# Two chained transformer blocks on one core: mixer layers reordered, one stream of differential attention, tables and copies released by other events

## Chip, cores and metric

One NeuronCore of a Trainium2 chip runs the whole program. The metric is the device time of one execution in microseconds, the median of several runs. Five engines work side by side, each through its own instructions in order: TensorE (PE; matmuls, with PEld for its weight loads), VectorE (DVE), ScalarE (ACT), GpSimd (POOL) and SyncE (SP), which here issues most of the DMAs. They meet through semaphores that the kernel sets and waits for by hand. TensorE's granted clock has two levels here, 2.4 GHz (1.00 in the profile) and 1.2 GHz (0.50).

## The reference, cut to what matters

Four layers run in a row over an image of 512 tokens and a context of 256, 1024 features each. Layer 0 is windowed attention with a sink, layer 1 a retention, layers 2 and 3 are layers of four mixers; every layer ends in a feed-forward. The last two, which most of the change is about:

```python
z = h @ w_in                                   # nine groups of 256 columns
u = gelu(group(z, G_AU)); v = rmsnorm(gelu(group(z, G_AV)))       # mixer a
mixed = einsum('hpq,bcqhd->bcphd', ws, v) + bs ; a = u * mixed
b = group(z, G_BB) * dwconv3(group(z, G_BC) * group(z, G_BX), w)  # mixer b
c = fft2(group(z, G_CF)).real                                     # mixer c
q, k = rope(group(z, G_DQ)), rope(group(z, G_DK)); v = group(z, G_DV)
s = einsum('bqhmd,bkhmd->bhmqk', q, k_all) * DIFF_QK ** -0.5      # mixer d
p = softmax(s); o = (p[:, :, 0] - lam * p[:, :, 1]) @ v_all
x = x + gt1 * (concatenate([a, b, c, rmsnorm(o, g) * (1 - lam_init)]) @ w_out)
```

Mixer d has four heads with two score maps each. Layer 2 computes it for the image's queries over all 768 keys and for the context's queries over the 256 keys of the context; layer 3 for the image alone.

## The kernel before

Activations lie transposed, features on the partitions: X, and HH and HL, the high and low halves of the normed input (eight tiles of 768 columns). Weights come in units of 128 output features; `plan_units` numbers all units of the program. SyncE loads unit u into WR[u % 2], ScalarE's `refill` writes its high half to WH (L665), VectorE's `refill` its low half to WL (L1011), and a product is three matmuls for each of eight input tiles: high by high, high by low, low by high (`product`, L302; `product_pair`, L315, for two units that follow a norm tile by tile; `product_rows`, L328, where tokens are the output's rows). A unit may be refilled only when the product two units before is done. PSUM is four tiles PS0 to PS3 of two banks each; `bank(PS, m)` is bank m of eight.

**First attention** (`attention` in every engine's program). 96 heads, one after the other: block b of queries, head n. In step i TensorE does the scores of head i (L434), the transposes of the probabilities of head i-3 into PS2 (L445) and, each second step, the values of two heads (L458). VectorE moves scores into SBUF and takes their maximum in one pass (L1210, printed as a custom instruction) and scales the head before (L1217, L1218). ScalarE, in step i, does the exponential of head i (L806) and then the copy of the transposed head i-3 out of PS2 (L823). The transposes of the next head wait for that copy.

**Retention** (L462 on). SyncE loads the tables and the distances only after the last tile of the norm (`h_lo`), and the weights after them.

**Mixers.** `mixers(l)`: two row units for AV into six banks, each with a gelu of its own (L883); then z units 0 to 11 and the two of DK into PS0 and PS1 by turns, each copied out by ScalarE (L889); then the spatial mixing; then two row units for DV into six banks, six copies (L909); then the Fourier mixer (`features` L558, `tokens` L568). GpSimd computes rope (L1514 to L1517). VectorE's in-order part before the stream is the AV norm, gate and convolution. The tables of a mixer layer wait for `h_lo` too, and unit 2's weights stand behind them in SyncE's queue. For the context the second Fourier table is loaded over the first.

**Differential attention.** Two blocks of eight heads over 768 keys (two query tiles each) and, in layer 2, one of eight over 256 keys. Each block is a pipeline of its own that is filled and drained: scores (L601) of both maps into PS0 and PS1, maximum (L1402) and its scaling (L1403) on VectorE, exponential on ScalarE straight from PSUM (L942), probabilities on VectorE (L1408 to L1411), transposes (L610), copy (L949), values (L619). A map's bank is free for the next head when its exponential is done. Behind the last block stands a norm over each head (`rsqrt`, `newton`, L1416), whose last halves (`mix_lo` 6 and 7) the first out product waits for.

## Time and profile before

| what | value |
|---|---|
| time, median of 3 runs | 3867.3 us (3866.22 to 3876.93) |
| the profiled execution: its time, its span | 3863.78 us, 3862.2 us |
| busy: PE, PEld, DVE, ACT, POOL | 91%, 73%, 45%, 32%, 8% of the span |
| instructions | 42880 |
| first attention / retention | from 236 to 471 us / from 1107 to 1763 us |
| mixers of layer 2: up to the stream / stream and norm | from 2144 to 2368 us / to 2515 us |
| mixers of layer 3: the same | from 3147 to 3326 us / to 3430 us |

How to read it: a wait is put down to the instruction that came last of those waited for. Idle time of an engine counts only where another waits for it. Matmuls are pipelined, and one that waits for its operands can be listed as long; their starts are more telling than their durations. A timeline merges neighbours of one line, and its count (x6) tells how many; a matmul of 32-bit floats appears as two in some counts.

### The profile page before, as it was taken

The page shows a single profiled execution, that of the slowest core. Times are in us where ns is not written, and L with a number is a line of the kernel's source. Part 1 is how long each engine was busy: PE and PEld are TensorE (multiplying, and loading weights), DVE is VectorE, ACT ScalarE, POOL GpSimd, SP SyncE. Part 2 cuts the span into 40 slices and gives each one's busy share as a digit, 9 for nine tenths or more (in the row PEclk, how much of TensorE's full clock was granted, in tenths as well). Part 3 has the DMA queues.
Part 4 walks back from the last instruction along what each step waited for, and adds up shares of the span by engine and source line. Part 5 has one row for each costly group of instructions (what it writes and reads, how often), then busy time and mean ns, then how long its engine had stood idle before and what let it go on. Part 6 is the DMA issues. An engine that isn't in the chain of part 4 may idle for free.

```text
span 3862.2 us, 42880 instructions
## 1 busy us (share of the span) xinstructions
PE 3519.3 (91%) x17952; PEld 2838.3 (73%) x17952; DVE 1750.9 (45%) x2605; ACT 1224.6 (32%) x1711; POOL 292.5 (8%) x361
## 2 busy tenths in 40 slices
PE   6967789999979999998999798989999979889998
PEld 3766578888866757656888685678888867567887
DVE  3555545433333433336756325546535432555343
ACT  4455542112232221224222323432212233344232
POOL 0100010000100000001001001010000010110001
PEclk8989899999999999998999897799999989899999
DMA  5400023423211212114544210013323322012222
GB/s 204 169 19 1 1 87 126 133 86 126 91 68 46 73 39 73 62 44 140 194 152 147 84 61 17 1 71 126 136 83 126 100 72 87 11 44 80 95 98 87
DMA packets 87903, 334.23 MB, mean 87 GB/s; under 512 B 11168, under 2 KB 14240, under 8 KB 83872
## 3 DMA queue, kind: packets, MB, share of 16 engines
q1 hardware_dynamic: 66544, 252.85, 18.5%
q0 software_dynamic: 21168, 78.65, 6.2%
q8 instruction: 142, 2.33, 0.2%
q14 instruction: 49, 0.40, 0.0%
HBM read 329.37 MB, written 2.10 MB: 86 GB/s over the span
## 4 chain that ended last, share of the span: by engine, by line
PE 86%; DVE 5%; ACT 5%; issue 2%; DMA 2%; SPq 0%; POOL 0%; ACTq 0%; DVEq 0%
PE PS L302 62%; PE PS L328 5%; PE PS L523 3%; PE PS L601 2%; PE PS L496 2%; PE PS L315 2%; PE PS L619 1%; PE PS L458 1%; PE PS L488 1%; PE PS L445 1%; PE PS L434 1%; PE PS L568 1%; PE PS L610 1%; DVE aP L1210 1%; DMA AR<-in_ada 1%
## 5 line engine op out<-in xcount | busy, mean ns | idle before, releaser
L302 PE MATMUL PS<-HH,WH 128*128 128x512 f32 (+1 forms) x3120 | 943.3, 357 | 69.2 <-ACT AV L883 33.4
L665 ACT ACTIVATE WH<-WR 128x1024 fp32r<-128x1024 f32 (+1 forms) x376 | 419.2, 1115 | 1735.4 <-PE PS L302 1466.1
L302 PE MATMUL PS<-HH,WL 128*128 128x512 f32 (+1 forms) x3120 | 937.7, 355 | 0.0
L302 PE MATMUL PS<-HL,WH 128*128 128x512 f32 (+1 forms) x3120 | 937.1, 355 | 0.0
L1011 DVE TENSOR_TENSOR WL<-WR,WH 128x1024 fp32r<-128x1024 f32 (+1 forms) x376 | 486.9, 1295 | 976.2 <-ACT WH L665 975.7
L302 PEld LDWEIGHTS PS<-HH,WH 128*128 128x128 f32 x3120 | 516.3, 190 | 161.2 <-ACT AV L883 33.8
L302 PEld LDWEIGHTS PS<-HL,WH 128*128 128x128 f32 x3120 | 514.8, 189 | 86.7 <-issue 2.2
L302 PEld LDWEIGHTS PS<-HH,WL 128*128 128x128 f32 x3120 | 515.3, 189 | 85.3
L302 PE MATMUL PS<-DH,WH 128*128 128x512 f32 (+1 forms) x1056 | 318.8, 356 | 0.0
L302 PE MATMUL PS<-DL,WH 128*128 128x512 f32 (+1 forms) x1056 | 318.7, 356 | 0.0
L302 PE MATMUL PS<-DH,WL 128*128 128x512 f32 (+1 forms) x1056 | 318.6, 356 | 0.0
L1137 DVE SCALAR_TENSOR_TENSOR X<-PS,MOD,X 128x512 f32<-128x512 f32 x96 | 60.5, 658 | 368.0 <-PE PS L302 368.0
L302 PEld LDWEIGHTS PS<-DL,WH 128*128 128x128 f32 x1056 | 174.3, 188 | 29.9
L302 PEld LDWEIGHTS PS<-DH,WH 128*128 128x128 f32 x1056 | 174.1, 188 | 30.2
L302 PEld LDWEIGHTS PS<-DH,WL 128*128 128x128 f32 x1056 | 174.0, 188 | 29.9
L1042 DVE SCALAR_TENSOR_TENSOR PS<-AT,CB 128x1024 f32<-128x1024 f32 x144 | 176.5, 1226 | 0.0
L328 PE MATMUL PS<-WH,HH 128*128 128x256 f32 (+1 forms) x416 | 142.2, 342 | 28.8 <-DVE HL L1069 15.8
L1487 POOL DMA_DIRECT2D AT<-in_adat x144 | 76.0, 528 | 1148.3 <-DVE AT L1042 574.5
L1479 POOL TENSOR_TENSOR WK<-WK,WK 128x768 f32<-128x768 f32 (+1 forms) x56 | 117.0, 2089 | 329.1 <-ACT WK L681 328.6
L328 PE MATMUL PS<-WL,HH 128*128 128x256 f32 (+1 forms) x416 | 140.8, 339 | 0.0
L328 PE MATMUL PS<-WH,HL 128*128 128x256 f32 (+1 forms) x416 | 140.8, 338 | 0.0
L740 ACT ACTIVATE DH<-WK 128x768 fp32r<-128x768 f32 (+1 forms) x88 | 65.0, 739 | 185.4 <-DVE WK L1128 185.4
(261 smaller groups left out, 3872.6 us busy)
## 6 DMA issues: line engine op xcount, KB each, us to landing
WR<-in_win SPq DMA_DIRECT2D x176, 512.0 KB, 3.5
AT<-in_adat POOLq DMA_DIRECT2D x144, 512.0 KB, 3.8
WR<-in_wdn SPq DMA_DIRECT2D x64, 704.0 KB, 4.0
WR<-in_wret SPq DMA_DIRECT2D x64, 512.0 KB, 3.6
WR<-in_zin SPq DMA_DIRECT2D x36, 512.0 KB, 3.5
AR<-in_ada SPq DMA_DIRECT2D x8, 1024.0 KB, 5.5
aV<-in_ada SPq DMA_DIRECT2D x8, 1024.0 KB, 4.9
aAR<-in_ada SPq DMA_DIRECT2D x8, 1024.0 KB, 6.6
```

Source lines behind the costliest of these rows:

```text
L302: mm = PE.matmul(dst[:, a:b], w[u % 2][:, k * P:(k + 1) * P], h[:, k, a:b], start=(k == 0 and i == 0), stop=(k == nk - 1 and i == 2))
L315: mm = PE.matmul(dst[v][:, a:b], w[(u + v) % 2][:, k * P:(k + 1) * P], h[:, k, a:b], start=(k == 0 and i == 0), stop=(k == KT - 1 and i == 2))
L328: mm = PE.matmul(dst(m), h[:, k0 + k, m * P:(m + 1) * P], w[u % 2][:, k * width:(k + 1) * width], start=(first and k == 0 and i == 0), sto ...
L496: mm = PE.matmul(d, M.rV[:, m, e * P:(e + 1) * P], M.rAT[:, m, :], start=(m == 0), stop=(m == 5))
L523: mm = PE.matmul(PS[half][:, 512 * v:512 * v + 512], wt[half][:, col:col + P], y[:, k, :], start=(k == 0 and i == 0), stop=(k == 3 and i = ...
L601: mm = PE.matmul(PS[mp][:, a:e], qs[r, h // 2, q * P:(q + 1) * P], M.DK[r, h // 2, k0 + a:k0 + e], start=True, stop=True, tile_position=(r ...
L665: AC.activation(M.WH[u % 2][:, 0:n], M.WR[u % 2][:, 0:n], COPY).then_inc(*on.up("w_hi", u))
L740: AC.activation(M.DH[:, j, 0:n], HF[:, 0:n], COPY).then_inc(*on.up("d_hi", (l, jj)))
L1011: VE.tensor_tensor(M.WL[u % 2][:, 0:n], M.WR[u % 2][:, 0:n], M.WH[u % 2][:, 0:n].bitcast(F32), ALU.subtract).then_inc(*on.up("w_lo", u))
L1042: i = VE.scalar_tensor_tensor((PS[3], M.AT[v % 3])[j][:, :], M.AT[v % 3][:, :], 1.0, M.CB[:, j, :], ALU.mult, ALU.mult, accum_out=MOD[:, l ...
L1479: PO.tensor_tensor(WK[2][:, 0:n], WK[2][:, 0:n], WK[k % 2][:, 0:n], ALU.add).then_inc(*on.up("square_summed", (tag, k)))
L1487: PO.dma_start(M.AT[v % 3][:, :], dram["adat"][l - 1, v]).then_inc(*on.up(f"mod_load{v % 3}", (l, v), 16))
```

## The change

It has six parts.
- **Order of units** in the mixer layers: `MIX` gives the order of the 14 units (u, Fourier input, q and k first, the convolution's last); DV's rows come ahead of the last six, the spatial mixing after six.
- **Rows two tiles to a bank**: AV's and DV's rows use `row_place`, banks 4 to 6, so three copies of 512 columns take the place of six of 256. The gelu of u is done in the copy out of PSUM. Rope moves from GpSimd to VectorE.
- **One stream**: the differential attention's blocks become one list of heads (`diff_heads`). VectorE's pass moves the scores to SBUF and takes their extreme in one (with `NIL`, a tile of zeros, as second operand); the exponential works in place in SBUF, and a bank is free when VectorE has read it. Scores of the two maps alternate, values of two heads too. The square sums behind it move into the first out product, after its third input tile.
- **Tables** of the retention and of the mixer layers wait for the last down product (and the last ada tile) and no longer for the norm. The context's Fourier table gets space of its own, in HL's last tiles; the second context's load moves to head 1 of the retention.
- **First attention**: in each step ScalarE copies the transposed head i-3 first and then does the exponential of head i; VectorE's low halves of the output come a step later.
- The layout of the z weights follows the new order of the units.

On ScalarE, in the first attention at 640 columns a step, before (aP is the exponential, aPT the copy; the last digits are buffers, aPT_93 to aPT_96 the four of a cycle, aP_89 to aP_92 likewise):

```order
L823 ACTIVATE aPT_95<-PS 128x640 [waits a_values,a_transposed]
L806 ACTIVATE aP_91,aRSM<-aP_91,aNM 128x641 [waits a_sink,a_max]
L823 ACTIVATE aPT_96<-PS 128x640 [waits a_values,a_transposed]
L806 ACTIVATE aP_92,aRSM<-aP_92,aNM 128x641 [waits a_sink,a_max]
L823 ACTIVATE aPT_93<-PS 128x640 [waits a_values,a_transposed]
L806 ACTIVATE aP_89,aRSM<-aP_89,aNM 128x641 [waits a_sink,a_max]
```

and now (aPT_94 to aPT_97, aP_90 to aP_93):

```order
L833 ACTIVATE aPT_97<-PS 128x640 [waits a_values,a_transposed]
L840 ACTIVATE aP_92,aRSM<-aP_92,aNM 128x641 [waits a_sink,a_max]
L833 ACTIVATE aPT_94<-PS 128x640 [waits a_values,a_transposed]
L840 ACTIVATE aP_93,aRSM<-aP_93,aNM 128x641 [waits a_sink,a_max]
L833 ACTIVATE aPT_95<-PS 128x640 [waits a_values,a_transposed]
L840 ACTIVATE aP_90,aRSM<-aP_90,aNM 128x641 [waits a_sink,a_max]
```

The two kinds alternated before and do so now; what moved is the place of a step's copy, from behind the exponential of head i to ahead of it (before: aP_92 and then aPT_93, the fourth and the first buffer; now aPT_97 and then aP_92, the fourth and the third).

On SyncE's queue at the start of mixer layer 2, behind the load of its second unit, before (dBD to WS are the first four of eleven tables; the third unit's load stands behind the last of them, before and now):

```order
L1552 DMA WR_53<-in_zin 128x1024 [waits w_lo]
L1561 DMA dBD<-in_bd 128x128 [waits h_lo]
L1561 DMA SLG<-in_subln 128x1
L1561 DMA LQ<-in_lambda 128x128
L1561 DMA WS<-in_gmlp_w 128x512
```

and now:

```order
L1589 DMA WR_54<-in_zin 128x1024 [waits w_lo]
L1598 DMA dBD<-in_bd 128x128 [waits ada_taken,product]
L1598 DMA SLG<-in_subln 128x1
L1598 DMA LQ<-in_lambda 128x128
L1598 DMA WS<-in_gmlp_w 128x512
```

The order is the same; the event that the first table waits for is another.

On VectorE, one head of the stream over 768 keys, before:

```order
L1402 TENSOR_REDUCE dNM<-PS 128x1 [waits d_scores]
L1403 TENSOR_SCALAR dNM<-dNM 128x1 [waits step]
L1402 TENSOR_REDUCE dNM<-PS 128x1 [waits d_scores]
L1403 TENSOR_SCALAR dNM<-dNM 128x1 [waits step]
L1408 RECIPROCAL dRL<-dRL 128x2 [waits d_exp]
L1409 TENSOR_TENSOR dRL<-dRL,LAM 128x1 [waits step]
L1410 TENSOR_SCALAR dP_157<-dP_157,dRL 128x768
L1411 SCALAR_TENSOR_TENSOR dP_157<-dP_159,dRL,dP_157 128x768 [waits step]
```

and now (ISA is the custom pass of L1210's kind, and the reading of its result):

```order
L1450 ISA dP_158,dNM<-PS,NIL 128x768 [waits d_scores,d_prob]
L1450 ISA dNM 128x1
L1450 ISA dP_159,dNM<-PS,NIL 128x768 [waits d_scores]
L1450 ISA dNM 128x1
L1457 RECIPROCAL dRL<-dRL 128x2 [waits d_exp]
L1458 TENSOR_TENSOR dRL<-dRL,LAM 128x1 [waits step]
L1459 TENSOR_SCALAR dP_157<-dP_157,dRL 128x768
L1460 SCALAR_TENSOR_TENSOR dP_157<-dP_160,dRL,dP_157 128x768 [waits step]
```

Two maxima and two scalings became two passes that also write dP; the rest of a head is unchanged.

The diff, cut to its core (what the code above shows and the change removes, places in SBUF, gate, convolution and weight layout are left out; the pieces are, in this order, of the module, TensorE, ScalarE, VectorE and SyncE):

```diff
+MIX = (0, 1, 8, 9, 10, 11, 12, 13, 2, 6, 4, 3, 7, 5)
+ROWS_AT, MIXED_AT = 8, 6
+def mix_units(l):
+    return [(p + 2 * (p >= ROWS_AT), p, z) for p, z in enumerate(MIX)]
+def diff_heads(l):
+    return [(q, h, 6 if q < 4 else 2, 0 if q < 4 else 4) for q in range(segments(l)[-1][1] // P) for h in range(4)]
+def row_place(ps, m):
+    return bank(ps, 4 + m // 2)[:, L * (m % 2):L * (m % 2) + L]
...
+        for at, p, z in mix_units(l):
+            if p == MIXED_AT:
+                PE.wait_ge(*on("av_normed", l))
+                PE.wait_ge(*on("table", f"mixers{l}"))
+                for t in (1, 0):
+                    for h in (2 * t, 2 * t + 1):
+                        for m in range(nt):
+                            mm = PE.matmul(mixed[t][64 * (h % 2):64 * (h % 2) + 64, m * P:(m + 1) * P],
+                                           M.AV[:, m, 64 * h:64 * h + 64], M.WS[:, h, :], start=True, stop=True)
+                    mm.then_inc(*on.up("mixed", (l, t)))
+            if p == ROWS_AT:
+                for t in range(2):
+                    PE.wait_ge(*on("mix_biased", (l, t)))
+                for v in range(2):
+                    product_rows(u + 2 + ROWS_AT + v, 4, 4 * v, L, range(6), place, v == 0, v == 1, None, True)
+            product(u + 2 + at, PS[p % 2], (HH, HL), KT, segs if z < 12 else ALL, ("z_copied", (l, MIX[p - 2])) if p > 1 else None)
 
...
+        heads = diff_heads(l)
...
+                rows = [slice(64 * (h % 2) + 32 * mp, 64 * (h % 2) + 32 * mp + 32) for mp in range(2)]
+                for a in range(0, w, 512):
+                    e = min(w, a + 512)
+                    for mp, r in enumerate(rows):
+                        if j and a == 0:
+                            PE.wait_ge(*on("d_max", (l, j - 1, mp)))
+                        mm = PE.matmul(PS[mp][:, a:e], M.Z[r, 10 + h // 2, q * P:(q + 1) * P], M.DK[r, h // 2, c0 + a:c0 + e],
+                                       start=True, stop=True, tile_position=(r.start, 0))
+                        if e == w:
+                            mm.then_inc(*on.up("d_scores", (l, j, mp)))
...
+            j = step - 4
+            if j >= 0 and j % 2 == 0:
+                q, h, nm, m0 = heads[j]
...
+                for m in range(nm):
+                    for g in range(2):
+                        mm = PE.matmul(out[64 * g:64 * g + 64, :], M.DV[:, m0 + m, 64 * (h + g):64 * (h + g) + 64],
+                                       M.dPT[(j + g) % 4][:, m, :], start=(m == 0), stop=(m == nm - 1))
+                mm.then_inc(*on.up("d_values", (l, j // 2)))
...
+        def square_sums():
+            for t in range(2):
+                PE.wait_ge(*on("o_squared", (l, t)))
+                PE.wait_ge(*on("d_turned", (l, len(heads) - 1)))
+                for a, b, _ in segs:
+                    mm = PE.matmul(PS[2 + t][:, a:b], M.dBD[:, :], (M.dP[0][0], M.dP[0][1])[t][:, a:b], start=True, stop=True)
+                mm.then_inc(*on.up("o_square_sum", (l, t)))
...
+            i = step - LAG
+            if 0 <= i < HEADS:
+                w = len(keys(i // 16)) * P
+                AC.wait_ge(*on("a_transposed", i))
+                if i > 3:
+                    AC.wait_ge(*on("a_values", (i - 4) // 2))
+                AC.activation(M.aPT[i % 4][:, 0:w], PS[2][:, 0:w], COPY).then_inc(*on.up("a_turned", i))
             i = step
             if i < HEADS:
...
+        for at, p, z in mix_units(l):
+            if p == ROWS_AT:
+                for v in range(2):
+                    refill(u + 4 + ROWS_AT + v)
+                AC.wait_ge(*on("product", u + 3 + ROWS_AT))
+                for i in range(3):
+                    AC.activation(flat(M.DV, 2 * i, 2 * i + 2), bank(PS, 4 + i), COPY).then_inc(*on.up("dv_copied", (l, i)))
+            refill(u + 4 + at)
+            AC.wait_ge(*on("product", u + 2 + at))
+            dst, w = (Z[:, z, 0:n], n) if z < 12 else (M.DK[:, z - 12, :], T)
+            AC.activation(dst, PS[p % 2][:, 0:w], GELU if z < 2 else COPY).then_inc(*on.up("z_copied", (l, z)))
+            if p == 5:
+                AC.wait_ge(*on("lambda_dots", l))
+                AC.activation(M.LAM[:, 0:2], M.LAM[:, 0:2], EXP).then_inc(*on.up("lambda_exp", l))
+            if p == 11:
+                middle(0)
...
+        heads = diff_heads(l)
+        for step in range(len(heads) + 4):
+            j = step - 3
+            if 0 <= j < len(heads):
+                nm = heads[j][2]
+                AC.wait_ge(*on("d_transposed", (l, j)))
+                if j > 3:
+                    AC.wait_ge(*on("d_values", (l, (j - 4) // 2)))
+                AC.activation(M.dPT[j % 4][:, 0:nm, :], PS[2][:, 0:nm * P].rearrange("p (a b) -> p a b", b=P),
+                              COPY).then_inc(*on.up("d_turned", (l, j)))
+            j = step
+            if j < len(heads):
+                w = heads[j][2] * P
+                for mp in range(2):
+                    p = M.dP[mp][j % (3 - mp)][:, 0:w]
+                    AC.wait_ge(*on("d_max", (l, j, mp)))
+                    AC.activation(p, p, EXP, bias=M.dNM[:, j % 4, mp:mp + 1], scale=-1.0,
+                                  accum_out=M.dRL[:, j % 4, mp:mp + 1]).then_inc(*on.up("d_exp", (l, j, mp)))
...
+        def rope(t):
+            q, rt, before = Z[:, 10 + t, 0:S] if t < 2 else M.DK[:, t - 2, 0:S], RT[:, :], {1: 0, 2: 1, 3: 2}.get(t)
+            VE.wait_ge(*on("z_copied", (l, 10 + t)))
+            if before is not None:
+                VE.wait_ge(*on("roped", (l, before)))
+            step(VE.stream_shuffle(rt, q, [i ^ 8 for i in range(32)]), ("rope_swapped", l, t))
+            VE.tensor_tensor(q, q, M.mCOS[:, :], ALU.mult)
+            step(VE.tensor_tensor(rt, rt, M.mSIN[:, :], ALU.mult), ("rope_sin", l, t))
+            VE.tensor_tensor(q, q, rt, ALU.add).then_inc(*on.up("roped", (l, t)))
...
+        for at, p, z in mix_units(l):
+            if p == ROWS_AT:
+                refill(u + 4 + ROWS_AT)
+                rope(2)
+                refill(u + 5 + ROWS_AT)
+                rope(3)
+            refill(u + 4 + at)
+            if p == 2:
+                lambda_dots()
+            if p == 5:
+                gate()
+            if p == 6:
+                rope(0)
+                lambda_rest()
+            if p == 7:
+                rope(1)
+            if p == 11:
+                conv(0)
...
+        for at in range(len(heads) + 1):
+            j = at
+            if j < len(heads):
+                w = heads[j][2] * P
+                if j > 2:
+                    VE.wait_ge(*on("d_transposed", (l, j - 3)))
+                if j > 1:
+                    VE.wait_ge(*on("d_prob", (l, j - 2)))
+                for mp in range(2):
+                    VE.wait_ge(*on("d_scores", (l, j, mp)))
+                    VE.tensor_tensor_reduce(M.dP[mp][j % (3 - mp)][:, 0:w], PS[mp][:, 0:w], M.NIL[:, 0:w], -(32 ** -0.5), 3e38,
+                                            ALU.add, ALU.min, M.dNM[:, j % 4, mp:mp + 1]).then_inc(*on.up("d_max", (l, j, mp)))
...
-    SP.wait_ge(*on("h_lo", ("1a", KT - 1)))
-    SP.dma_start(M.X[:, :, S:T], dram["xc2"].rearrange("p (k t) -> p k t", k=KT)).then_inc(*on.up("x_load", 1, 16))
+    SP.wait_ge(*on("product", FIRST["down", 0, 1] + KT - 1))
+    SP.wait_ge(*on("ada_taken", (1, NV - 1)))
...
+        if h == 1:
+            SP.wait_ge(*on("h_lo", ("1a", KT - 1)))
+            SP.dma_start(M.X[:, :, S:T], dram["xc2"].rearrange("p (k t) -> p k t", k=KT)).then_inc(*on.up("x_load", 1, 16))
...
-        SP.wait_ge(*on("h_lo", (f"{l}a", KT - 1)))
+        SP.wait_ge(*on("product", FIRST["down", l - 1, 1] + KT - 1))
+        SP.wait_ge(*on("ada_taken", (l, NV - 1)))
...
-            SP.wait_ge(*on("dft_tokens", (l, 0, 1)))
-            SP.dma_start(M.CN[:, :, 0, :], dram["dft256"]).then_inc(*on.up("dft", (l, 1), 16))
+            SP.wait_ge(*on("product", u + 17))
+            SP.dma_start(M.CC[:, :, :, :], dram["dft256"].rearrange("p q (m k) -> p q m k", m=2)).then_inc(*on.up("dft", (l, 1), 16))
```

## Rows read from the trace of the kernel before

**Rows 1.** Waits of TensorE, whole span: line <- releaser: us in total, times, longest.

```profile
PE PS L445 <- ACT aPT L823: 63.1, 54, 2.8
...
PE PS L302 <- ACT AV L883: 33.4, 2, 18.5
...
PE PS L558 <- ACT DV L909: 13.2, 2, 7.0
...
PE PS L302 <- DVE HL L1378: 7.9, 3, 4.1
...
PE PS L568 <- DMA CN<-in_dft: 2.7, 1, 2.7
```

**Rows 2.** Timeline, first attention: start, us, engine, line, out<-in, count [idle before <-releaser].

```profile
321.20 0.73 PE L445 MATMUL PS<-aID,aP 128*128 128x128 f32 x5
...
321.69 0.89 PE L434 MATMUL PS<-aK,aQS 128*128 128x256 f32 x6
...
322.33 0.83 ACT L806 ACTIVATE aP<-aP,aNM 128x641 f32<-128x641 f32 x1 [2.32 <-DVE aNM L1210]
...
323.16 0.68 ACT L823 ACTIVATE aPT<-PS 128x640 f32<-128x640 f32 x1
...
323.99 0.74 PE L445 MATMUL PS<-aID,aP 128*128 128x128 f32 x5 [1.41 <-ACT aPT L823]
...
324.66 1.31 PE L458 MATMUL PS<-aPT,aV 128*64 128x128 f32 x20
...
326.66 0.73 PE L445 MATMUL PS<-aID,aP 128*128 128x128 f32 x5
```

**Rows 3.** Timeline, start of the retention.

```profile
1141.19 1.06 ACT L665 ACTIVATE WH<-WR 128x1024 fp32r<-128x1024 f32 x1 [11.55 <-DMA WR<-in_wret]
...
1143.56 1.01 PE L302 MATMUL PS<-HH,WH 128*128 128x512 f32 x2 [11.21 <-DVE WL L1011]
```

**Rows 4.** Timeline, end of layer 1's feed-forward and SyncE's tables.

```profile
2142.76 0.75 DVE L1137 SCALAR_TENSOR_TENSOR X<-PS,MOD,X 128x512 f32<-128x512 f32 x1 [5.32 <-PE PS L302]
...
2167.91 0.33 SPq L1561 DMA_DIRECT2D dBD<-in_bd  x1
```

**Rows 5.** Chain that ended last, mixer layer 2: start, us, what.

```profile
2173.51 10.58 DMA WR<-in_zin
...
2392.00 2.87 PE PS L601 x8
...
2394.87 1.47 PE PS L610 x6
...
2396.34 2.75 PE PS L619 x12
```

**Rows 6.** Timeline, differential attention of layer 2, at full clock.

```profile
2408.25 0.96 DVE L1402 TENSOR_REDUCE dNM<-PS 128x1 f32<-128x768 f32 x1 [2.22 <-PE PS L601]
...
2408.95 1.52 PE L619 MATMUL PS<-dPT,DV 128*64 128x128 f32 x12
...
2409.31 0.95 DVE L1402 TENSOR_REDUCE dNM<-PS 128x1 f32<-128x768 f32 x1
...
2412.21 0.95 DVE L1402 TENSOR_REDUCE dNM<-PS 128x1 f32<-128x768 f32 x1
```

**Rows 7.** Windows: stretch, length, busy of PE PEld DVE ACT POOL, granted clock, DMA.

```profile
2368.00:2420.00 52.00, 46.24 (x192) 29.68 (x191) 32.29 (x67) 23.34 (x43) 0.00 (x0) 0.67 0.00 0
...
2420.00:2470.00 50.00, 45.93 (x201) 29.99 (x200) 31.39 (x64) 21.84 (x42) 0.00 (x0) 0.69 0.00 1
...
2470.00:2515.00 45.00, 37.73 (x160) 23.97 (x158) 24.25 (x72) 21.01 (x53) 0.00 (x0) 0.71 0.00 1
...
3326.00:3375.00 49.00, 43.64 (x216) 28.68 (x216) 32.26 (x66) 22.60 (x43) 0.00 (x0) 0.79 0.00 0
...
3375.00:3430.00 55.00, 46.81 (x225) 31.53 (x225) 35.94 (x72) 28.58 (x51) 0.00 (x0) 0.84 0.00 1
```

**Rows 8.** VectorE groups, first attention: busy us, mean ns | idle before.

```profile
L1210 DVE CUSTOM_DVE_ANT_0 aP<-PS,aMK,aSK 128x640 f32<-128x640 f32 x32 | 28.2, 881 | 32.3 <-PE PS L434 32.2
```

More of the change, by code:

```diff
@@ L289, in tensor_program, with product @@
     PS, HH, HL, WH, WL = M.PS, M.HH, M.HL, M.WH, M.WL
-    def product(u, dst, src, nk, segs, after=None, ready=None):
+    def product(u, dst, src, nk, segs, after=None, ready=None, between=None):
         PE.wait_ge(*on("w_lo", u))
@@ L297, in product @@
         for k in range(nk):
+            if between and k == 3:
+                between()
             if ready:
@@ L318, in product_pair, with product_rows @@
                     mm.then_inc(*on.up("product", u + v))
-    def product_rows(u, nk, k0, width, tiles, dst, first, last, ready=None):
+    def product_rows(u, nk, k0, width, tiles, dst, first, last, ready=None, paired=False):
         PE.wait_ge(*on("w_lo", u))
@@ L328, in product_rows @@
                 mm = PE.matmul(dst(m), h[:, k0 + k, m * P:(m + 1) * P], w[u % 2][:, k * width:(k + 1) * width],
-                               start=(first and k == 0 and i == 0), stop=(last and k == nk - 1 and i == 2))
+                               start=(first and k == 0 and i == 0 and not (paired and m % 2)),
+                               stop=(last and k == nk - 1 and i == 2 and not (paired and m % 2 == 0)))
         mm.then_inc(*on.up("product", u))
@@ L530, in mixers @@
         u = FIRST["zin", l]
+        place = lambda m: row_place(PS, m)
         for v in range(2):
-            product_rows(u + v, 4, 4 * v, L, range(nt), lambda m: bank(PS, m)[:, 0:L], v == 0, v == 1,
-                         ("h_lo", f"{l}a"))
-        PE.wait_ge(*on("av_gelu", (l, nt - 1)))
-        for i in range(12):
-            product(u + 2 + i, PS[i % 2], (HH, HL), KT, segs, ("z_copied", (l, i - 2)) if i > 1 else None)
-        for i in range(2):
-            product(u + 14 + i, PS[i], (HH, HL), KT, ALL, ("z_copied", (l, 10 + i)))
@@ L549, in mixers @@
[L549 to L552 removed]
+            product_rows(u + v, 4, 4 * v, L, range(nt), place, v == 0, v == 1, ("h_lo", f"{l}a"), True)
+        mixed = [PS[3], PS[2]]
+        for at, p, z in mix_units(l):
[14 more added lines that the diff above has]
+            product(u + 2 + at, PS[p % 2], (HH, HL), KT, segs if z < 12 else ALL, ("z_copied", (l, MIX[p - 2])) if p > 1 else None)
@@ L622, in mixers @@
-        last = 2 if n > S else 1
-        for t in range(2):
-            PE.wait_ge(*on("o_squared", (l, t)))
-            PE.wait_ge(*on("d_out", (l, last, 1)))
-            PE.wait_ge(*on("d_turned", (l, last, 7)))
-            for a, b, _ in segs:
-                mm = PE.matmul(PS[2 + t][:, a:b], M.dBD[:, :], (M.dP[0][0], M.dP[0][1])[t][:, a:b], start=True, stop=True)
-            mm.then_inc(*on.up("o_square_sum", (l, t)))
+                tokens(t, S, lambda q, m: M.CC[:, q, m, :], 2, L)
@@ L958, in mixers @@
-        last = 2 if n > S else 1
+        heads = diff_heads(l)
+        for step in range(len(heads) + 4):
+            j = step - 3
+            if 0 <= j < len(heads):
+                nm = heads[j][2]
[4 more added lines that the diff above has]
+                              COPY).then_inc(*on.up("d_turned", (l, j)))
+            j = step
+            if j < len(heads):
[5 more added lines that the diff above has]
+                                  accum_out=M.dRL[:, j % 4, mp:mp + 1]).then_inc(*on.up("d_exp", (l, j, mp)))
+            j = step - 5
+            if j >= 0 and j % 4 == 2:
+                q = heads[j][0]
+                AC.wait_ge(*on("d_values", (l, j // 2)))
+                AC.activation(M.OD[:, :, q * P:(q + 1) * P], bank(PS, 6 + q % 2)[:, 0:2 * P].rearrange("p (t q) -> p t q", t=2),
+                              COPY).then_inc(*on.up("d_out", (l, q)))
@@ L959, in mixers @@
         N = [*M.dP[0], M.dP[1][0]]
-        AC.wait_ge(*on("d_out", (l, last, 1)))
+        AC.wait_ge(*on("d_out", (l, heads[-1][0])))
         for t in range(2):
@@ L1200, in attention @@
             stack(0, g)
-        for at in range(HEADS + LAG + 4):
+        for at in range(HEADS + LAG + 5):
             i = at
@@ L1233, in retention @@
         T1, T2, DC, TMP, DS = M.rAT[:, 0, :], M.rAT[:, 1, :], M.rDC[:, :], M.rTMP, M.rDS
-        VE.wait_ge(*on("table", "retention"))
-        VE.memset(M.rON[:, :], 1.0 / 512).then_inc(*on.up("step", "rON"))
         def rope(h, what, pa, pb, dst):
@@ L1250, in retention @@
             VE.wait_ge(*on("product", u + 1))
+            if h == 0:
+                VE.wait_ge(*on("table", "retention"))
+                VE.memset(M.rON[:, :], 1.0 / 512).then_inc(*on.up("step", "rON"))
             rope(h, 0, PS[0], PS[1], M.rQ)
```

278 lines of the change are left out of this document (84 added, 194 removed).

## The prediction

> **What bounds the kernel now.** I read the waits of TensorE first: they say where it stands still and which instruction ended each wait. Four lines hold most of it: 63.1 us in the first attention behind ScalarE's copies at L823, 33.4 us at the starts of the two mixer layers behind the gelu of AV, 13.2 us behind the copies of DV, 2.7 us behind a table; 7.9 us at the heads of the out projections come on top [rows 1]. Then the timeline of each place, for what is really late there. Last the windows, because TensorE's granted clock is not the same everywhere: in the differential attention it is 0.67 to 0.71 of full speed on average in layer 2 and 0.79 to 0.84 in layer 3 [rows 7], that is, one part of the stretch at 1.2 GHz and the rest at 2.4.
>
> **First attention: copies first.** At 321.20 TensorE transposes a head's probabilities, done at 321.93. The copy that frees their bank starts only at 323.16, since on ScalarE the exponential of a later head (322.33) stands ahead of it. The next transposes wait 1.41 us for that copy and start at 323.99 [rows 2]. In the changed order the copy can start at 321.95 and ends after its 0.68 us at about 322.65; the scores in between end at 322.58. So the transposes start at about 322.7 instead of 323.99: 1.28 of 1.41 us go, 91%. What is delayed is the exponential, from 322.33 to 322.67. Its result is wanted three heads later, and two heads now take 5.46 us (321.20 to 326.66 [rows 2]), so it has 8 us and, at the new pace, still 6: nothing. If that cover were gone, 0.34 us a head would come back, 33 us for 96 heads. 91% of 63.1 is 57 us. I take off 7 for the ten places where ScalarE stacks queries between copies, whose delay stays. **-50**, bounds -40 and -60. VectorE's low halves, one step later, lie in the same slack.
>
> **Retention.** The tables are loaded after the norm, the next weights queue behind them, ScalarE gets those only at 1141.19 after 11.55 us of idle time, and TensorE stands 11.2 us until 1143.56 [rows 3]. The changed queue waits for the last down product (and the last ada tile, which is earlier) instead, so all of it lands under the norm. What is late next is the conversion of that unit, which needs the buffer that the first product of the pair frees: 1.06 us on ScalarE [rows 3] and about as long on VectorE, against some 0.7 us of matmuls of the pair's other half that are left by then. So about 1.5 us of wait stay. **-10** (bounds -8 and -12). The 1 MB load of the second context moves to head 1, ahead of that head's weights on SyncE's queue; those are wanted two products later, some 10 us: 0 to +2, and I take 0.
>
> **Mixers up to the streams.** The same with the norms of layers 2 and 3: the down product ends just before 2142.76, the tables start at 2167.91 [rows 4], and the next weights land 10.6 us after their issue at 2173.51 [rows 5]. On the new condition all of this is 25 us sooner, and the weights land near 2159, ahead of the norm's end (where the tables start now). The gelu no longer stands between rows and units either: rows go two tiles to a bank into PS2 and PS3, units into PS0 and PS1. The 33.4 us go but for a microsecond. DV's rows come ahead of six units and their three copies lie under those; the 13.2 us become the copy of the last unit, 1 us a layer. The context's table has its own space in HL's tail: -2.7. Rope on VectorE (a shuffle and three passes over 512 columns, each 0.65 us by the 0.96 of a maximum over 768 [rows 6]) is 2.6 us beside a conversion of about 1.1; a unit has 24 matmuls at least, 6 us at full clock by the 1.01 us that two take at half of it [rows 3]. It fits, and so do gate and convolution: nothing. After each of the vanished waits the matmuls now restart at half clock (that same row), which I price at 6 together. 33.4 + 13.2 + 2.7 - 3 + 6: **-52** (bounds -45 and -58).
>
> **Differential attention.** At 1.2 GHz a head costs TensorE 2.87 us for scores, 1.47 for transposes and 2.75 for values, 7.1 in all [rows 5], and VectorE waits. At 2.4 GHz the values take 1.52 and VectorE is the bound: it starts heads at 2408.25 and 2412.21, 3.96 us apart [rows 6]. The pass that replaces maximum and scaling also moves the scores to SBUF. The trace has it at 640 columns as 881 ns [rows 8], so 1.06 us or a little less at 768; from one maximum to the next it is 1.06 now (2408.25 to 2409.31). VectorE's work for a head stays at 4.0 to 4.1. What goes is its idle time at starts and ends of blocks, and half of TensorE's time for values, since two heads now run side by side, as in the first attention (1.31 us for 20 instructions [rows 2], so 1.6 for 24).
> At 2.4 GHz throughout, a layer then costs VectorE's busy time, one start, one end and the norm behind it. Layer 2: 147 us from 2368 to 2515, busy 32.3+31.4+24.3 = 88, idle 59 [rows 7]. Of the idle time there stay, as estimates, 5 at the start, 2 at the end and 9 in the norm: -43. Layer 3: 104 us, busy 32.3+35.9 = 68, idle 36 [rows 7], of which 15 stay: -21.
> At 1.2 GHz two heads cost TensorE 2 x (2.87+1.47) + 3.2 = 11.9, against 8.1 on VectorE: +4 for two heads. The start, where TensorE waits for VectorE's first passes, is as long as before, so the clock will fall there as it does now. How long it stays down is the open size: the mean clocks (twice what is missing from 1, times the length) say 34, 31 and 26 us in layer 2's three windows, 21 and 18 in layer 3's two. I take one such stretch a layer, 25 us or two pairs: +8 each. **-35** and **-13**; bounds -43 and -8, -21 and +11.
> That values of two heads side by side gain anything goes against a rule of the Trainium skill (TensorEngine Tiling (Array Packing), PSUM Bottleneck): tiling speeds up the matmuls but not the emptying of PSUM, which can become the bound. At 2.4 GHz the rows above are that case; at 1.2 GHz they are not, TensorE being the full engine. By the rule alone a pair at 1.2 GHz would keep its 14.2 us, and the time would be 3716.
> The square sums now stand behind three steps of the first out product instead of ahead of it. The 7.9 us at its head [rows 1] wait for the norm on ScalarE and VectorE, which the move doesn't shorten: 0 to +1, and I take 0.
>
> **Sum.** -50-10-52-35-13 = -160, against the profiled execution's 3863.8 (span 3862.2): 3704. The median of the runs is 3867.3, 3.5 above it, so 3707. Errors of 10, 2, 6, 12 and 12 that don't hang together make this case 3687 to 3727.
>
> **Rivals.** (1) The streams stay at 1.2 GHz from start to end. For it: layer 2's windows are more than half at that level, the one with the context's block too [rows 7]. Against: layer 3's heads wait on VectorE in the same way and run two thirds of the time at full speed. Layer 2 then keeps -43+4x8+3 = -8 and layer 3 -21+4x8 = +11: instead of -48 it is +3, time 3758. The Trainium skill (TensorE: Matmul & The Clock Gate, HAM oscillation) says that a kernel whose matmuls come in bursts between waits falls back to the lower rate again and again; by that rule this is the case to expect.
> (2) In the first attention the exponential, now behind the copy, is late, and the wait for the copy turns into one for probabilities: 33 us come back, 3740. Against it: the three heads of lead.
> (3) The clock stays at 2.4 GHz in both streams: 16 us better, 3691. For it: one start a layer instead of two or three. Against: the start itself.
> (4) Slower than before: copy ahead of exponential ties each head to the one before it. Then a head costs a whole chain: scores 0.89, reduction 0.88, exponential 0.83, transposes 0.73, copy 0.68 [rows 2, 8] and, as an estimate, 0.9 for reading the sum and scaling, 4.9 us in all against 2.73 now (half of 5.46); +2.2 at 640 columns, on average perhaps 1.6, so +155 for 96 heads instead of -50: 3912. It decides from the point where one head's chain is longer than the three heads of lead, 6 us at the new pace. It is 4.9.
>
> **How the numbers follow.** Forecast 0.64, (1) 0.14, (2) 0.10, (3) 0.09, (4) 0.03. The range goes from (3) with some error to (1): 3682 to 3758. About 0.3% (12 us) is what a measurement here can tell from no change; all cases but (4) are far beyond it, and only several losses together would end there: faster 0.95, same 0.02, slower 0.03.
>
> **What would show it.** In the first attention the waits for the copies fall from 63 to under 12 us, and no other wait of TensorE there passes 10. No wait over 2 us at the start of the retention, and none over 2 between a mixer's rows and its stream. In each stream one stretch of about 25 us at half clock, then heads 4.0 to 4.2 us apart with VectorE busy throughout. Wrong would be: half clock to the end of a stream; heads of 5 us at full clock (a dearer pass); conversions of weights that come late because VectorE turns rope or convolves first.

## The result and the profile after

The changed kernel takes 3691.6 us in the median (3685.3 to 3699.4, four runs), the kernel before 3871.0 beside it: a ratio of 0.9537, interval 0.9508 to 0.9565. Measured again with other runs it is 3691.3 and 0.9536 (0.9512 to 0.9559). The profiled execution has a span of 3684.0 us against 3862.2. Times below are medians, and "over" or "under" is against 3691.3 unless something else is named; the kernel before, measured beside each group of runs, took 3867.6 to 3868.4 us.

The span is 178.2 us shorter. The stretches, from the starts and ends of the matmuls in the two traces:

| stretch | before, us | after, us | change | forecast |
|---|---|---|---|---|
| first attention, first scores to first out product | 234.6 | 171.2 | -63.4 | -50 |
| from the last down product to the retention's product of [rows 3] | 38.2 | 29.1 | -9.2 | -10 |
| rest of the retention | 617.5 | 612.9 | -4.5 | 0 |
| mixers, last down product to first scores, layers 2 and 3 | 226.9 + 181.2 | 197.0 + 148.6 | -62.5 | -52 |
| first scores to end of the out product, layer 2 | 207.2 | 177.1 | -30.2 | -35 |
| the same, layer 3 | 144.8 | 136.2 | -8.6 | -13 |
| all else | | | +0.2 | 0 |

Waits of TensorE after the change, whole span (line <- releaser: us in total, times, longest), where [rows 1] has 63.1, 33.4, 13.2, 7.9 and 2.7:

```profile
PE PS L470 <- ACT aPT L833: 12.4, 38, 1.1
...
PE PS L326 <- DVE HL L1427: 11.0, 4, 3.3
PE PS L632 <- ACT dPT L969: 10.7, 9, 3.4
...
PE PS L326 <- DVE WL L1037: 5.4, 3, 2.1
...
PE PS L581 <- ACT Z L931: 1.9, 2, 1.0
```

The waits for AV, DV and CN are gone altogether; in the place of DV's 13.2 stand 1.9 for the last unit's copy, and the retention starts after a wait of 2.1 for its weights (the longest in the fourth line) instead of 11.2. The waits inside the first out products, 7.9 before, are 11.0 now. Of the signs that the prediction named, two are missed by a little: the copies' 12.4 is not under 12, and the retention's 2.1 not under 2. Between a mixer's rows and its stream no wait is over 1.0. The timeline of the first attention after, two heads at 640 columns (start, us, engine, line):

```profile
302.61 0.73 PE L470 MATMUL PS<-aID,aP 128*128 128x128 f32 x5
...
303.37 0.71 ACT L833 ACTIVATE aPT<-PS 128x640 f32<-128x640 f32 x1 [1.15 <-PE PS L470]
...
303.97 0.82 ACT L840 ACTIVATE aP<-aP,aNM 128x641 f32<-128x641 f32 x1
...
304.22 0.74 PE L470 MATMUL PS<-aID,aP 128*128 128x128 f32 x5 [0.23 <-ACT aPT L833]
...
306.88 0.73 PE L470 MATMUL PS<-aID,aP 128*128 128x128 f32 x5
```

The copy (L833) now starts when the transposes (L470) end, the exponential (L840) follows it, and the next transposes wait 0.23 us instead of 1.41 [rows 2]. Two heads take 4.27 us instead of 5.46.

The windows of the two streams after (the columns of [rows 7]; the granted clock is the third figure from the end):

```profile
2262.00:2288.00 26.00, 24.53 (x94) 13.92 (x94) 17.59 (x39) 12.19 (x24) 0.00 (x0) 0.61 0.00 0
2288.00:2352.00 64.00, 56.01 (x381) 35.21 (x381) 52.94 (x144) 40.61 (x94) 0.00 (x0) 0.89 0.00 1
3156.00:3182.00 26.00, 24.05 (x91) 13.57 (x90) 17.75 (x38) 12.41 (x24) 0.00 (x0) 0.61 0.00 0
3182.00:3230.00 48.00, 41.05 (x268) 25.78 (x266) 39.77 (x88) 29.47 (x58) 0.00 (x0) 0.88 0.00 1
```

Each stream starts with one stretch of 20 us at half clock (2 x 0.39 x 26). Behind it the clock is mostly full but not always: 0.89 of 64 us and 0.88 of 48 are another 14 and 12 us at half. VectorE's passes there, at full clock:

```profile
2287.88 0.96 DVE L1450 CUSTOM_DVE_ANT_0 dP<-PS,NIL 128x768 f32<-128x768 f32 x1 [2.98 <-PE PS L620]
...
2288.76 0.95 DVE L1450 CUSTOM_DVE_ANT_0 dP<-PS,NIL 128x768 f32<-128x768 f32 x1
...
2291.71 0.96 DVE L1450 CUSTOM_DVE_ANT_0 dP<-PS,NIL 128x768 f32<-128x768 f32 x1
...
2295.62 0.96 DVE L1450 CUSTOM_DVE_ANT_0 dP<-PS,NIL 128x768 f32<-128x768 f32 x1 [0.22 <-PE PS L620]
```

Heads are 3.83 and 3.91 us apart, a little under the 4.0 to 4.1 of the prediction: from one pass to the next it is 0.88 us, where a maximum with its scaling took 1.06 [rows 6]. That holds only at full clock; where it has fallen, a head comes up to 5.8 us after the one before it.

### The profile page after: what moved, and what is told of

The parts are those of the page before. It is cut to its first block, busy times and chain, and to the rows that moved or that the text cites. A ratio compares the mean times of both kernels' runs of the same rounds, so it can differ in the third digit from the quotient of the medians.

```text
span 3684.0 us, 42824 instructions
## 1 busy us (share of the span) xinstructions
PE 3449.4 (94%) x17952; PEld 2782.0 (76%) x17952; DVE 1743.7 (47%) x2627; ACT 1214.7 (33%) x1696; POOL 255.6 (7%) x337
## 4 chain that ended last, share of the span: by engine, by line
PE 89%; DVE 4%; ACT 4%; issue 1%; DMA 1%; SPq 0%; POOL 0%; DVEq 0%; ACTq 0%
PE PS L326 65%; PE PS L352 6%; PE PS L548 3%; PE PS L521 2%; PE PS L339 2%; PE PS L620 1%; PE PS L470 1%; PE PS L513 1%; PE PS L483 1%; PE PS L645 1%; PE PS L459 1%; PE PS L591 1%; DMA AR<-in_ada 1%; PE PS L632 1%; DVE dP L1450 1%
## 5 line engine op out<-in xcount | busy, mean ns | idle before, releaser
L326 PEld LDWEIGHTS PS<-HH,WH 128*128 128x128 f32 x3120 | 514.6, 189 | 122.4 <-issue 16.6
```

Source lines behind the costliest of these rows:

```text
L326: mm = PE.matmul(dst[:, a:b], w[u % 2][:, k * P:(k + 1) * P], h[:, k, a:b], start=(k == 0 and i == 0), stop=(k == nk - 1 and i == 2))
```

## The experiments

**The changed kernel again** stands beside the others.

> The changed kernel itself, beside which the others are read. Every theory expects its 3691.6 us (3685 to 3699).

It took 3691.3 us. Its profile differs from the first one mainly in layer 2's stream with the out product, 183.6 us instead of 177.1, so the streams' entries in the table are good to some 6 us.

**First attention: waits or clock?** My theory was that 50 of the 63 us are waits and 13 the clock. Two runs. In the changed kernel the order put back, on ScalarE and with VectorE's low halves a step earlier again:

```diff
-            i = step - LAG
-            if 0 <= i < HEADS:
...
-                AC.activation(M.aPT[i % 4][:, 0:w], PS[2][:, 0:w], COPY).then_inc(*on.up("a_turned", i))
             i = step
...
                         "p (a b) -> p a b", b=P), COPY).then_inc(*on.up("o_hi", (b, t // 4)))
+            i = step - LAG
+            if 0 <= i < HEADS:
...
+                AC.activation(M.aPT[i % 4][:, 0:w], PS[2][:, 0:w], COPY).then_inc(*on.up("a_turned", i))
```

And in the kernel before, useless matmuls ahead of the transposes of every second head, where TensorE waited, into the place that the next values overwrite:

```diff
+                    for _ in range(6):
+                        PE.matmul(bank(PS, 6 + tt // 4)[:, tt % 4 * P:(tt % 4 + 1) * P], M.aID[:, :], M.aID[:, :], start=True, stop=True)
```

> The changed kernel with the first attention put back: in each step the exponential of head i first, then the copy of head i-3, and VectorE's low halves a step earlier. Theory: the first attention got 63 us shorter, 50 of them by the waits for the copies and 13 by TensorE's clock, which no longer falls there because TensorE no longer stands still; both come back with the order, so +63 us, the waits for copies at 60 us or more, and about 34 us at half clock between 256 and 470 us. Rival: only the waits hang on the order, and the 13 us come from another part of the change: +50 us, and no half clock in that stretch.

> The kernel before, with six matmuls of 128x128 that nobody reads in every second step of the first attention, put where TensorE waits 1.41 us for a copy. The output is unchanged. Theory (the clock gives 13 of the 63 us): two heads at 640 columns still take 5.46 us, but the stretches at half clock between 256 and 470 us go, and the kernel is 13 us faster than before, 3855. Rival (the 13 us come from shorter work per head): the time stays as before, 3867 to 3871, whatever the clock does.

With the order put back: 3758.0 us, 67 over; the first attention takes 234.5 us again, the waits for the copies are at 63.3, and the clock is back at 0.93. The windows from 256 us to near the end of the first attention: kernel before, copies last, changed kernel, before with useless matmuls:

```profile
256.00:466.00 210.00, 149.05 (x1341) 123.57 (x1339) 125.01 (x373) 124.22 (x284) 17.24 (x87) 0.93 0.00 1
```

```profile
256.00:466.00 210.00, 149.00 (x1340) 123.48 (x1338) 124.98 (x374) 124.28 (x284) 17.39 (x87) 0.93 0.00 1
```

```profile
256.00:402.00 146.00, 131.57 (x1296) 109.96 (x1292) 118.81 (x360) 117.82 (x274) 17.19 (x84) 1.00 0.01 2
```

```profile
256.00:462.00 206.00, 197.23 (x1883) 176.25 (x1883) 125.77 (x374) 124.52 (x285) 17.14 (x87) 0.99 0.01 1
```

So the whole 63 us and the clock hang on the two moves put back here, ScalarE's order and the step of VectorE's low halves; the two were not run apart. The useless matmuls raise the clock from 0.93 to 0.99 without changing the order, and 3860.9 us against 3868.4 is 0.9977 (0.9960 to 0.9994): 2 to 15 us less, 7.5 in the middle and not 13. In its trace the first attention takes 230.1 us, 4.5 less than before. The trace says why it is not more: pairs of heads that fell on half clock go from 7.02 and 7.73 us to 5.38, while at 256 columns, where the wait is shorter than six matmuls, some pairs grow, from 3.01 to 3.67. That the clock pays is shown; that it pays 13 is not. Pair by pair, steady pairs at full clock give 48 us (8 pairs each of 1.04, 1.17, 1.17, 1.06, 0.79 and 0.79 in the six blocks); some 9 more come from pairs that had been at half clock, and the rest from the pairs in which ScalarE also stacks queries (5.94 us before, 4.28 after).

**Mixer starts: weights behind tables, or gelu?**

```diff
-    SP.wait_ge(*on("product", FIRST["down", 0, 1] + KT - 1))
-    SP.wait_ge(*on("ada_taken", (1, NV - 1)))
+    SP.wait_ge(*on("h_lo", ("1a", KT - 1)))
...
-        SP.wait_ge(*on("product", FIRST["down", l - 1, 1] + KT - 1))
-        SP.wait_ge(*on("ada_taken", (l, NV - 1)))
+        SP.wait_ge(*on("h_lo", (f"{l}a", KT - 1)))
```

> The changed kernel, but the tables of the retention and of the mixer layers wait for the norm again. Theory: at the starts of the mixer layers it was the weights behind the tables that TensorE waited for, not the gelu of AV. Then the retention starts 9 us later, and from the last down product to the first unit after the rows it takes 45.5 us again instead of 31.1 (layer 2) and 26.9 (layer 3): +14 and +19, with 3 to 8 us of half clock after the waits: +45 to +50 us in all. Rival: the gelus and their six evictions were the wait, and they stay gone: only the retention's 9 us come back.

3728.3 us, 37 over. The timeline of the changed kernel with late tables, layer 2 (SPq is the DMA queue; a merged row is as long as its loads together):

```profile
2100.14 0.33 SPq L1598 DMA_DIRECT2D dBD<-in_bd  x1
...
2105.26 27.20 SPq L1589 DMA_DIRECT2D WR<-in_zin  x5
...
2115.87 1.06 ACT L692 ACTIVATE WH<-WR 128x1024 fp32r<-128x1024 f32 x1 [16.75 <-DMA WR<-in_zin]
...
2118.24 1.01 PE L326 MATMUL PS<-HH,WH 128*128 128x512 f32 x2 [12.69 <-DVE WL L1037]
...
2119.46 1.57 ACT L910 ACTIVATE AV<-PS 128x512 f32<-128x512 f32 x3
```

and of the changed kernel:

```profile
2065.04 0.33 SPq L1598 DMA_DIRECT2D dBD<-in_bd  x1
...
2070.16 28.86 SPq L1589 DMA_DIRECT2D WR<-in_zin  x4
...
2096.09 0.52 PE L326 MATMUL PS<-HH,WH 128*128 128x512 f32 x2
```

With early tables the first unit follows the rows without a wait. With late ones TensorE stands 12.7 us (16.6 in layer 3, 8.5 at the retention) for the conversion of weights that land late, and this although the gelu (L910) comes after that matmul, which does not wait for it. So 29 of the 33.4 us that [rows 1] puts down to the gelu were the weights; the gelus stood behind the conversion on ScalarE's queue and only reported last. In the kernel before, layer 2:

```profile
2182.86 1.06 ACT L665 ACTIVATE WH<-WR 128x1024 fp32r<-128x1024 f32 x1 [15.96 <-DMA WR<-in_zin]
...
2186.48 1.76 ACT L883 ACTIVATE AV<-PS 128x256 f32<-128x256 f32 x6
...
2188.29 1.01 PE L302 MATMUL PS<-HH,WH 128*128 128x512 f32 x2 [14.91 <-ACT AV L883]
```

The expected 45 to 50 were 8 to 13 too many. Some 4 of them are what the gelus and their six evictions had cost themselves: from the last down product to the first unit it now takes 43.3 and 43.7 us, not 45.5. Another 3 are the retention's, whose start comes 6.5 us later and not 9; the rest is open.

**DV's place, and the square sums.**

The first kernel moves DV's rows, the second the sums:

```diff
-ROWS_AT, MIXED_AT = 8, 6
+ROWS_AT, MIXED_AT = 13, 6
```

```diff
-        return square_sums
+        square_sums()
...
-        project(l, segments(l), mixers(l))
+        mixers(l)
+        project(l, segments(l))
```

> The changed kernel with DV's rows ahead of the last unit instead of ahead of the last six. Theory (three wide copies and any unit behind them are enough, some 2 us under 8): the same time, 3691, and no wait for DV's copies. Rival (DV's rows need the place: their copies stand behind late conversions on ScalarE, or the shuffles and passes of rope that go with them delay the last unit's conversion): a wait of 3 us or more at the start of the Fourier features in each layer, 3697 and up.

> The changed kernel with the square sums of the differential attention ahead of the first out product, as before, instead of behind its third step. Theory (the norm on ScalarE and VectorE is what the product waits for either way): the same time, 3691, within 2 us. Rival (three steps of the product, 3 to 5 us, are now done while the squares are made): +3 us a layer or more, 3697 and up.

DV's rows ahead of the last unit alone: 3691.0 us, and no wait for DV: the one unit left behind the copies covers them. Square sums ahead: 3686.9 us, ratio 0.9523 (0.9498 to 0.9548). That is 0.1% under the changed kernel and within the spread; it speaks against a gain from the move and shows no loss. With the sums ahead the waits inside the out products are 7.5 us and 2.5 more stand before the sums; with the sums inside they are the 11.0 above.

**Values of two heads side by side.**

```diff
-                for m in range(nm):
-                    for g in range(2):
+                for g in range(2):
+                    for m in range(nm):
```

> The changed kernel with the values of two heads one after the other, all key tiles of the first and then all of the second, instead of alternating between the two halves of the array. Theory (alternating halves run side by side): the 24 matmuls of a pair take 3.0 us instead of 1.53 at full clock and 5.5 instead of 2.83 at half; at half clock that is on the path, +5 us a layer, and at full clock TensorE's work for a pair goes from 6.3 to 7.8 us, just over VectorE's 7.7: +10 to +20 us, 3701 to 3711. Rival (the emptying of PSUM sets the rate either way): the 24 matmuls take 1.5 us still, and the time stays at 3691. The Trainium skill (TensorEngine Tiling (Array Packing), PSUM Bottleneck) speaks for the rival.

3711.5 us, 20 over (0.9599, 0.9580 to 0.9618), the upper end of the theory. The values of two heads, changed kernel, at half and at full clock:

```profile
2283.09 2.83 PE L645 MATMUL PS<-dPT,DV 128*64 128x128 f32 x24
2292.44 1.53 PE L645 MATMUL PS<-dPT,DV 128*64 128x128 f32 x24
```

and one after the other:

```profile
3190.06 4.49 PE L645 MATMUL PS<-dPT,DV 128*64 128x128 f32 x24
3200.76 2.45 PE L645 MATMUL PS<-dPT,DV 128*64 128x128 f32 x24
```

Side by side they are 1.6 times as fast at either clock. By the rule of the Trainium skill (TensorEngine Tiling (Array Packing), PSUM Bottleneck) the emptying of PSUM could have become the bound. The trace does not agree here: with the values apart VectorE waits 30.7 us for scores in layer 2's stream instead of 17.3, and behind the start the clock is 0.85 instead of 0.89. So about half of the 39 us that the streams gained hangs on this alternation. What the single list of heads and the new pass gave, each by itself, was not run.

**The clock in the streams.** Useless matmuls into a free part of the values' bank: 17 in the first four steps, then three more in every second step.

```diff
+            if step > 3 and step % 2 == 0:
+                fill(l, heads, step - 4, 3)
...
+            if step < 4:
+                fill(l, heads, 0, (5, 4, 4, 4)[step])
```

> The changed kernel with 17 matmuls of 128x256 that nobody reads in the first four steps of each stream of differential attention, where TensorE waits for VectorE's first passes. The output is unchanged. Theory (the clock sets the start): the 20.5 us at half clock at the start of each stream go, the sixth head's pass begins about 20 us after the first scores instead of 25.9, 6 us a layer: 12 us less, 3679. Rival (the start is as long as VectorE's passes and the way from scores to probabilities make it): at most 2 us less a layer, or none, whatever the clock does.

> The same, and three more such matmuls ahead of the scores in every second step of the stream. Theory: the stretches of 3.4 us at half clock that stand in each stream after its start (three to five a layer, 1.9 us lost in each) go too, 5 us a layer: 22 us less than the changed kernel in all, 3669, with heads 3.84 us apart from the fifth on. Rival: VectorE sets the pace and the added matmuls delay the scores that it waits for: heads over 4 us apart, and the time is over that of the kernel with the start alone.

3676.8 and 3671.2 us, 15 and 20 under. From first scores to the first out product layer 2 takes 97.3 us in the changed kernel, 90.7 with a filled start and 88.1 filled throughout; layer 3 takes 82.3, 76.5 and 71.7. The windows with the streams filled throughout:

```profile
2267.00:2289.00 22.00, 21.93 (x130) 14.68 (x130) 17.45 (x38) 12.16 (x24) 0.00 (x0) 1.00 0.00 1
2289.00:2350.00 61.00, 56.41 (x441) 38.38 (x442) 53.56 (x148) 40.49 (x94) 0.00 (x0) 1.00 0.00 1
3151.00:3174.00 23.00, 22.80 (x137) 15.71 (x134) 18.60 (x39) 12.11 (x24) 0.00 (x0) 1.00 0.00 1
3174.00:3220.00 46.00, 41.88 (x335) 28.88 (x334) 40.85 (x92) 31.02 (x60) 0.00 (x0) 1.00 0.01 1
```

The clock is full in all four, and the time goes with it. The filled start saves 6.6 and 5.8 us, the filling behind it 2.6 and 4.8. These are differences of single profiles: in the seven whose streams are those of the changed kernel the same stretches take 97.3 to 101.3 and 80.0 to 82.3 us. Up to the sixth head's pass the start alone saves 4.9 and 5.1 us (21.0 and 21.3 after the first scores instead of 25.9 and 26.4); the expected 6 was a little too much.

**The same elsewhere.** Behind the sum of squares of each norm, 14 times in the first kernel and 9 times in the other two; the last has them in the streams, ahead of the retention's out products and ahead of the last two steps of the mixers' first out products as well.

```diff
+            if tag != "final":
+                for _ in range(14):
+                    PE.matmul(PS[0][:, 0:512], M.ONE[:, :], M.CAC[:].rearrange("p a b c -> p (a b c)"), start=True, stop=True)
```

> The changed kernel with 14 matmuls of 128x512 that nobody reads behind the sum of squares of each of seven norms, in the 7.9 us that TensorE waits there for the normed input. The output is unchanged. Theory (the clock falls because TensorE stands still, and that costs time only in the matmuls that follow): the seven stretches of 6.8 to 10.3 us at half clock go, of which about 5 us of work each ran at half speed, 2.5 to 3.5 us a norm: 17 to 25 us less than the changed kernel, 3666 to 3674. Rival: the clock falls at these places for another reason than the standing still, and nothing changes, or the added matmuls end late and delay the product: 3691 or more.

> As the kernel with matmuls behind the seven norms, with nine instead of 14. There 14 took 11.4 us (0.82 us each) in a wait of 7.9, so that the product behind each norm began 3.5 us late, 25 us in all; the kernel was 15 us over the changed one, so 10 us came back from the clock. Theory (that is the whole of it): nine take 7.4 us, end in time, and the 10 us stay: 3681. Rival (the clock gains nothing there, and the 15 us had other grounds): 3691, with the stretches at half clock behind the norms as in the changed kernel.

> The changed kernel with matmuls that nobody reads in most places where TensorE stands still and its clock then falls: in the streams (-20 us measured), nine behind each of seven norms (-10), five ahead of each retention head's out product (its wait is 5.6 us, and 6.8 us at half clock follow), two and three ahead of the last two steps of the mixer layers' first out product (waits of 2.4 and 3.3 us, 10.2 and 6.8 us at half clock follow). The output is unchanged. Theory (each place gives back the half of the work done at half clock behind it): -2 us for each of four heads and -3 for each of two products on top: 3691 - 20 - 10 - 8 - 6 = 3647. Rival (TensorE held busy throughout is granted less somewhere else, or the gains don't add): 3660 or more.

Fourteen behind each norm: 3706.3 us, 15 over. In the timeline they outlast the wait:

```profile
2077.47 12.18 PE L386 MATMUL PS<-CAC,ONE 128*128 128x512 f32 x28
2089.09 0.69 PE L352 MATMUL PS<-WH,HH 128*128 128x256 f32 x1
```

The rows of layer 2 begin 15.0 us after the last down product instead of 11.4. I had sized the filling by one instruction, and each of these matmuls is two (x28). Nine: 3688.2 us, 3 under and not 10, which is within the spread of the changed kernel. The trace shows more: of the seven products behind the norms three end 1.4 to 2.5 us sooner than in the two profiles of the changed kernel, some 6 us together, and four change by half a microsecond at most. At two of these four the wait was 5.6 us and not 7.9, and nine matmuls outlast it (7.2 and 7.4). The other two, at the retention and at layer 3's mixers, end 23.3 to 23.5 us after the sums with none, nine or fourteen, whenever they begin; that something else ends last there, most likely the norm's last tiles, is argued. The theory holds in kind and is worth at most 6 us. All places together: 3657.7 us, 0.9450 (0.9427 to 0.9474), 34 under the changed kernel, whose interval it does not touch: the fastest of all. The measured time is 11 us over the expected 3647: in the trace the norms give some 6 of 10, the out products 5 of 6, and the retention's products 1.5 to 4 of 8.

## Why the prediction was right, and where it was off

The measured 3691.6 us lie in the range and in the forecast case's own (3687 to 3727), 15 below its middle. It equals the figure of rival (3), but not its mechanism: the streams did fall to half clock as forecast, and their term came out smaller, not larger. The sum fits better than its terms: the first attention and the mixers lie beyond their own bounds by 3 and 4.5 us, and that the streams fall 9 us short offsets a part of that, which is luck. Point by point:

- **First attention, -50, came to -63.** The step from 1.41 us of wait to next to none was right (0.23 are left), and no exponential is late (waits for probabilities are 2.1 us in all): rival (2) and the slower rival (4) did not occur. Two sizes were wrong. The 7 us taken off for stacking should not have been, and the clock was left out: the kernel before ran at 0.93 there, and I priced the clock in the streams and behind the mixers' waits only.
- **Retention, -10, came to -9**, with 2.1 us of wait left where I had 1.5. The rest of that layer became 4.5 us shorter, 1.9 of them in the first product, which no longer restarts at half clock. The other 2.7 need not be the change's: in the second profile of the changed kernel the rest takes 615.7 us, 2.8 more than in the first. The moved load shows no cost.
- **Mixers, -52, came to -62.5**, beyond the bound of -58. For 34 of them the mechanism is shown by the late tables, which bring the two stretches back to 212.3 and 167.1 us; for DV's copies, the gelus and the context's table it is read from the waits that are gone. Two waits of the kernel before that I had passed over went as well:

```profile
PE PS L545 <- DVE AV L1339: 2.5, 2, 2.1
...
PE PS L328 <- DVE mT L1354: 1.4, 1, 1.4
```

What is left, some 6 us, is mostly more clock than the 6 that I gave it. In these stretches TensorE was busy at half clock for 31.1 us before and for 10.1 after; half of the difference, 10.5 us, is an estimate of what came back.
- **Streams, -35 and -13, came to -30 and -9.** The stretch at the start was right in kind and a third too dear: forecast 25 us at half clock and 8 us lost, measured 20 us, and 6.6 and 5.8 saved by filling it. The step that failed is "one such stretch a layer", with VectorE busy throughout behind it: VectorE does set the pace, but TensorE stands still often enough that its clock falls again and again for a moment, which costs 3 to 5 us a layer. The Trainium skill (TensorE: Matmul & The Clock Gate, HAM oscillation) tells of a clock that falls again and again in the waits between bursts. I gave that all of rival (1) or nothing; the trace shows it in between, at 0.89 and 0.88 behind the start.
- **Square sums, DV's copies, rope on VectorE: nothing**, as forecast. The first two were run; for rope there is only the trace, in which no matmul of the mixers waits for a conversion of weights.

## What to carry to other kernels

Price a vanished wait with the clock that comes back with it: read the granted clock of every stretch in which a wait goes, not only of the one that seems odd. When a wait is put down to an instruction that itself stood in a queue, look for what that queue waited for; moving a load's trigger (here the tables) can be worth more than the instruction that the row names. Where TensorE waits beside a full VectorE, matmuls for nobody that fit in the wait keep its clock up and can pay, but measure their length first.

## What was not expected of the hardware

Between 530 and 650 us TensorE runs the same products without a pause, at granted clock 1.00 in both profiles of the changed kernel, and yet not equally fast. First profile and second (`x` counts the matmuls):

```profile
530.00:650.00 120.00, 120.00 (x682) 103.99 (x681) 61.37 (x84) 25.68 (x28) 7.88 (x15) 1.00 0.36 123
```

```profile
530.00:650.00 120.00, 120.00 (x695) 104.97 (x694) 61.23 (x83) 27.23 (x30) 7.95 (x15) 1.00 0.40 128
```

That is 1.9% fewer in the same time. It costs the first feed-forward 3.2 us in some executions and none in others: in the fourteen profiles of this case its products take 536.0 us ten times and 532.8 four times and never anything between. Wherever it is slow, it is so in its first 180 us, where 256 matmuls take 45.2 us instead of 44.4. It may be a part of the 12 us between executions of one kernel. What it hangs on was not tried.
